# A quarter of the tokens through row gathers in a product-key expert layer

## The chip, the cores and the metric

The kernel runs on one core of a Trainium2 chip. The metric is the device time of one launch in microseconds (us), 2985.03 us as the median of three runs before the change.

## What is computed

The whole layer is an adaptive-LN transformer layer over 512 latent tokens and 256 context tokens of width 1024: a token mixer (Fourier branch and gated DeltaNet branch), a post-norm, and then product-key retrieval of single-neuron experts ("PEER"), with a last post-norm. The change lies in the experts. Each token has 8 heads that pick 16 of 16384 experts each, so 128 experts per token:

```
expert_idx = take_along_axis(cand_i, best_j)          # per token 8 heads x 16 experts
gate = softmax(best_s)
act  = gelu(einsum('td,thkd->thk', h, expert_u[expert_idx]), approximate=False)
coef = gate * act
out  = einsum('thk,thkd->td', coef, expert_v[expert_idx])
x    = post_norm(x, mx[:, 5] * out, ln_g[l, 1], ln_b[l, 1])
```

All arrays are float32. `expert_u` and `expert_v` have 16384 rows of 1024 values (4 KB a row).

## The kernel before

The kernel is one program with a hand-written order for each engine (SP and ACT issue the loads and stores, PE multiplies, ACT, DVE and POOL work element by element), tied together by counting semaphores.

Products with weights use a split: a weight tile of 128 x 1024 values comes from DRAM into `raw` (2 slots), ACT casts it to `w_hi`, POOL subtracts to get `w_lo` (`lo`, L837; 4 slots each), and each product takes three matmuls (`mm3`, L471: hi x hi, lo x hi, hi x lo). The load of tile n + 2 is issued by SP when `split_done` says that POOL is through with tile n (`next_w`). The cast of a tile into a slot of the ring waits until PE is through with the tile four before it.

The experts are computed densely: not 128 per token, but all 16384 for all 512 tokens, 128 tiles of 128 experts each. The stages, in order:

1. Query: 16 rounds. A round multiplies one tile of the query weights and one tile of `peer_u` by the 512 tokens (`lat_hi`, `lat_lo`), 24 matmuls each, then multiplies queries by sub-keys. DVE takes the top 16 of each (L1221 to L1252).
2. Candidates: four blocks of 128 tokens. DVE combines the two key halves, takes the top 16 again, and writes expert indices and gates (`eidx`); ACT gives the exponential after its `U_CD` u tiles of the block (L785). Meanwhile PE runs 8 u tiles a block (`U_CD = 8`); it then waits for `cd_out` and transposes `eidx` (L1709).
3. Marks: 64 rounds of 8 tokens. For each token DVE writes two marks of 128 columns (L1318: 1 where the row of the expert grid is, L1319: the gate where the column is), PE multiplies the two (L1720) into a 128 x 128 table of gates, ACT copies it to `gs`, and it is stored to DRAM (`g_dram`). One u tile runs in each round. The result of every u tile goes through gelu (`gu`) and to DRAM (`gu_dram`).
4. The last 16 u tiles.
5. Values: 128 tiles. DVE multiplies gelu values and gates (`cf`, L1329), ACT and DVE split the product (`c_hi`, `c_lo`), PE multiplies the tile of `peer_v` by it into 8 banks (experts' width as rows, 512 tokens as columns): 24 matmuls of 512 columns. `gl` and `gq` bring gelu values and gates back from DRAM, 1 MB each for four tiles.
6. The end: ACT scales the banks into `acc`, PE transposes it back, DVE adds the residual (L1353), normalizes, and SP stores the output.

## Time and profile before

| | |
|---|---|
| median of 3 runs | 2985.03 us (2984.15 to 2985.14) |
| the profiled execution, its own time | 2981.59 us |
| its span, first to last instruction | 2979.8 us |
| PE busy | 2728.1 us (92%) |
| PE weight loads busy | 2233.9 us (75%) |
| DVE busy | 1433.3 us (48%) |
| POOL busy | 967.3 us (32%) |
| ACT busy | 917.5 us (31%) |
| DMA, mean over the span | 354.24 MB, 119 GB/s |
| share of the span after the query stage begins (1277 us) | 57% |

Matmuls are pipelined, so the mean duration of one (about 0.4 us) is not what it costs. The cost is the distance from one start to the next, which the timeline gives. A busy share is a mean over stages with different limits, so the table is only the way in.

### The profile page before, as it was taken

How to read it: one execution, taken by the hardware profiler on the slowest of the kernel's cores; microseconds unless marked ns; L12 is line 12 of the kernel's file. 1: busy time of each engine (PE TensorE's matmuls, PEld its weight loads, DVE VectorE, ACT ScalarE, POOL GpSimd, SP SyncE). 2: the span in 40 equal slices, each digit the busy share in tenths (PEclk: the TensorE clock that was granted, in tenths of full speed). 3: DMA queues.
4: the chain of work that ended last, by engine and by line, in shares of the span. 5: the costliest groups of instructions: out<-in, count | busy, mean ns of one | idle time of the engine just before them, and what ended most of it. 6: DMA issues, size and time to landing. Idle time of an engine off the chain costs nothing.

```text
span 2979.8 us, 40461 instructions
## 1 busy us (share of the span) xinstructions
PE 2728.1 (92%) x13688; PEld 2233.9 (75%) x13688; DVE 1433.3 (48%) x3468; ACT 917.5 (31%) x1217; POOL 967.3 (32%) x425
## 2 busy tenths in 40 slices
PE   6888889889888999599989999999999999999996
PEld 2687677677667677478877788888878888888885
DVE  2656647647655111434678677777402222222223
ACT  3322221321321222233333445555322222222221
POOL 1212211221220244234444333333344444444441
PEclk8999899899898999799999999999999999999998
DMA  5100100110111223133343355555565555555551
GB/s 208 64 29 28 56 35 34 43 39 31 42 56 36 70 100 102 47 102 111 116 137 115 104 179 204 168 166 209 181 206 179 183 198 182 181 200 179 181 203 50
DMA packets 130236, 354.24 MB, mean 119 GB/s; under 512 B 10640, under 2 KB 43536, under 8 KB 128784
## 3 DMA queue, kind: packets, MB, share of 16 engines
q1 hardware_dynamic: 127648, 312.76, 31.7%
q10 hardware_dynamic: 2544, 40.90, 3.5%
q8 instruction: 28, 0.46, 0.1%
q14 instruction: 16, 0.13, 0.0%
HBM read 284.41 MB, written 69.21 MB: 119 GB/s over the span
## 4 chain that ended last, share of the span: by engine, by line
issue 45%; PE 27%; POOL 18%; DVE 6%; ACT 2%; DMA 0%; POOLq 0%; DVEq 0%; SPq 0%; ACTq 0%
POOL w_lo L840 17%; PE bank L473 4%; PE bank L475 4%; PE bank L474 4%; DVE cv L1014 2%; PE bank L1491 2%; PE bank L1506 2%; PE bank L1499 2%; PE bank L1366 1%; PE bank L1432 1%; DVE dY L1052 1%; PE bank L1422 1%; PE bank L1615 1%; PE bank L1534 1%; PE bank L1541 1%
## 5 line engine op out<-in xcount | busy, mean ns | idle before, releaser
L840 POOL TENSOR_TENSOR w_lo<-raw,w_hi 128x1024 fp32r<-128x1024 f32 x344 | 850.2, 2473 | 1717.8 <-ACT w_hi L709 864.2
L473 PE MATMUL bank<-lat_hi,w_hi 128*128 128x512 f32 x1568 | 631.8, 403 | 22.1 <-DMA sk<-sub_keys 8.1
L475 PE MATMUL bank<-lat_hi,w_lo 128*128 128x512 f32 x1568 | 614.9, 392 | 0.0
L474 PE MATMUL bank<-lat_lo,w_hi 128*128 128x512 f32 x1568 | 614.4, 392 | 0.0
L473 PE MATMUL bank<-c_hi,w_hi 128*128 128x512 f32 x1024 | 405.8, 396 | 6.8 <-ACT gu L766 6.8
L474 PE MATMUL bank<-c_lo,w_hi 128*128 128x512 f32 x1024 | 405.7, 396 | 0.0
L475 PE MATMUL bank<-c_hi,w_lo 128*128 128x512 f32 x1024 | 405.5, 396 | 0.0
L473 PEld LDWEIGHTS bank<-lat_hi,w_hi 128*128 128x128 f32 x1568 | 297.6, 190 | 81.8 <-issue 23.8
L475 PEld LDWEIGHTS bank<-lat_hi,w_lo 128*128 128x128 f32 x1568 | 296.4, 189 | 64.7
L474 PEld LDWEIGHTS bank<-lat_lo,w_hi 128*128 128x128 f32 x1568 | 297.8, 190 | 56.7
L1318 DVE TENSOR_SCALAR oh<-cst,eidT 128x128 f32<-128x128 f32 x512 | 247.1, 483 | 105.2 <-PE bank L1720 103.3
L1329 DVE TENSOR_TENSOR cf<-gl,gq 128x512 f32<-128x512 f32 x128 | 100.8, 788 | 333.6 <-DMA gq<-g_dram 330.1
L709 ACT CAST w_hi<-raw 128x1024 fp32r<-128x1024 f32 x244 | 254.3, 1042 | 0.0
L810 ACT CAST c_hi<-cf 128x512 fp32r<-128x512 f32 x128 | 79.3, 620 | 513.7 <-PE bank L475 502.7
L473 PEld LDWEIGHTS bank<-c_hi,w_hi 128*128 128x128 f32 x1024 | 193.0, 188 | 53.8 <-issue 7.2
L475 PEld LDWEIGHTS bank<-c_hi,w_lo 128*128 128x128 f32 x1024 | 192.9, 188 | 46.5
L474 PEld LDWEIGHTS bank<-c_lo,w_hi 128*128 128x128 f32 x1024 | 192.9, 188 | 46.5
L1335 DVE TENSOR_TENSOR c_lo<-cf,c_hi 128x512 fp32r<-128x512 f32 x128 | 88.3, 690 | 279.0 <-ACT c_hi L810 278.9
L1319 DVE TENSOR_SCALAR oh<-cst,eidT 128x128 f32<-128x128 f32 x512 | 189.6, 370 | 0.0
L1720 PEld LDWEIGHTS bank<-oh 128*128 128x128 f32 x1024 | 125.7, 194 | 8.2 <-issue 3.4
L796 ACT COPY gs<-bank 128x512 f32 x128 | 129.3, 1119 | 0.1
L1720 PE MATMUL bank<-oh 128*128 128x128 f32 x1024 | 126.4, 277 | 3.0 <-DVE oh L1319 3.0
(291 smaller groups left out, 3338.2 us busy)
## 6 DMA issues: line engine op xcount, KB each, us to landing
raw<-w SPq DMA_DIRECT2D x344, 512.0 KB, 3.7
gu_dram<-gu SPq DMA_DIRECT2D x128, 256.0 KB, 3.9
g_dram<-gs ACTq DMA_DIRECT2D x8, 4096.0 KB, 12.4
gl<-gu_dram SPq DMA_DIRECT2D x32, 1024.0 KB, 6.5
gq<-g_dram SPq DMA_DIRECT2D x32, 1024.0 KB, 9.1
ada<-w_ada SPq DMA_DIRECT2D x32, 512.0 KB, 4.0
ada_a<-w_ada SPq DMA_DIRECT2D x8, 512.0 KB, 8.7
xin<-x SPq DMA_DIRECT2D x4, 512.0 KB, 12.1
```

Source lines behind the costliest of these rows:

```text
L473: nc.tensor.matmul(out, hi, rh, start=start, stop=False)
L474: nc.tensor.matmul(out, hi, rl, start=False, stop=False)
L475: return nc.tensor.matmul(out, lo, rh, start=False, stop=stop)
L709: nc.scalar.copy(w_hi[:, q % RING, :], raw[:, q % RAW, :]).then_inc(hi_done, 1)
L796: nc.scalar.copy(gs[:, j, :, bass.ds(t * 32 + (8 * w + 4 * z), 4)].rearrange("p i t -> p t i"), bank[z][:, :].rearrange("p (t i) -> p t i" ...
L810: nc.scalar.copy(c_hi[:, y % 4, :], cf[:, y % 2, :]).then_inc(ch, 1)
L840: nc.gpsimd.tensor_sub(w_lo[:, slot, :], raw[:, slot % RAW, :], w_hi[:, slot, :].bitcast(F32)).then_inc(split_done, 1)
L1318: nc.vector.tensor_scalar(first_, iota, eidT[:, 0, col], None, ALU.is_equal).then_inc(oh_done, 1)
L1319: nc.vector.tensor_scalar(oh[:, z, w, 1, :], iota, eidT[:, 1, col], eidT[:, 2, col], ALU.is_equal, ALU.mult).then_inc(oh_done, 1)
L1329: nc.vector.tensor_tensor(cf[:, x % 2, :].rearrange("p (g t) -> p g t", t=GTOK), gl[:, slot, x % 4, :].rearrange("p (g t) -> p g t", t=GTO ...
L1335: nc.vector.tensor_sub(c_lo[:, x % 4, :], cf[:, x % 2, :], c_hi[:, x % 4, :].bitcast(F32)).then_inc(cl, 1)
L1720: last = mm(bank[z][:, v * P:(v + 1) * P], oh[:, z, v, 1, :], oh[:, z, v, 0, :], start=True, stop=True)
```

## The change

The first 128 of the 512 tokens no longer go through the dense stages. For them POOL issues 256 indirect gathers (`fetch`): gather q brings, for each of the 128 tokens, the row of its q-th expert (128 rows of 4 KB, 512 KB), first 128 times from `peer_u`, then 128 times from `peer_v`, into a ring of `ROWS = 8` buffers. DVE takes the dot product of each u row with the token (`dot`, the token rows lie in PSUM, `pair`), ACT applies one gelu to all of them (`e_act`), and DVE adds each v row times its coefficient into `pair` in PSUM (`add_row`).

The other 384 tokens (`DT`) go through the dense stages: u matmuls have 384 columns. The candidate blocks take 12 u tiles each (`U_CD = 12`), the marks stage has 48 rounds, the tail again 16. In the marks stage DVE reads its iota from a PSUM bank (`bank[5]`), not from SBUF, and writes the first mark of four tokens in one instruction. In the values stage the roles are swapped: coefficients (128 tokens) are the weights and a tile of `peer_v` is what moves, 512 columns at a time, 18 matmuls a tile, so the sums lie with tokens as rows. The end needs no scaling by ACT and no transposes; DVE multiplies by a gate row (`g2row`, made before by two matmuls with ones) and adds the residual. Coefficients and gelu values come back in transfers of 768 KB.

```diff
+DT = SEQ - P
+U_CD = 12
-X_END = X_G + SEQ // 8
+X_END = X_G + DT // 8
+ROWS = 8
+DOT_G = 8 * (DT // 32)
+V_BANK = ((0, 1), (4, 5), (6, 7))
...
+            def fetch(q):
+                if q == 0:
+                    pool.wait_ge(row_id, 1)
+                if q >= ROWS and q % 2 == 0:
+                    pool.wait_ge(row_used, q - ROWS + 2)
+                table = A["peer_u"] if q < P else A["peer_v"]
+                nc.gpsimd.indirect_dma_start(rows[:, q % ROWS, :], None, table,
+                                             bass.IndirectOffsetOnAxis(ap=e_row[:, q % P:q % P + 1], axis=0)
+                                             ).then_inc(row_in[q % ROWS // 2], 16)
+            def tile_of(q):
+                if q < ROWS:
+                    return T_U - 2 * PH + X_CD + 2 * U_CD + RING
+                n = q - ROWS
+                if n < DOT_G:
+                    return T_U - 2 * PH + X_G + n // 2 + RING + 1
+                if n < P:
+                    return T_U - 2 * PH + X_END + RING + 1 + (n - DOT_G) // 3
+                return T_V + n - P + RING + 1
+            q = 0
+            for n in range(T_QUERY + RING, T_ALL):
+                lo(n % RING, n + 1)
+                while q < 2 * P and tile_of(q) <= n:
+                    fetch(q)
+                    q += 1
...
-            with dve.Fori(0, SEQ // 8) as t:
-                for z in range(2):
-                    dve.wait_ge(g_mm, t * 2)
-                    for w in range(4):
-                        col = bass.ds(t * 8 + (4 * z + w), 1)
-                        first_ = oh[:, z, w, 0, :]
-                        nc.vector.tensor_scalar(first_, iota, eidT[:, 0, col], None, ALU.is_equal).then_inc(oh_done, 1)
-                        nc.vector.tensor_scalar(oh[:, z, w, 1, :], iota, eidT[:, 1, col], eidT[:, 2, col],
-                                                ALU.is_equal, ALU.mult).then_inc(oh_done, 1)
+            def dot(i, q):
+                if q % 2 == 0:
+                    dve.wait_ge(row_in[q % ROWS // 2], i * 32 + (q // ROWS + 1) * 32)
+                row = rows[:, q % ROWS, :]
+                nc.vector.scalar_tensor_tensor(row, row, 1.0, pair[:, :], ALU.mult, ALU.mult,
+                                               accum_out=e_dot[:, bass.ds(i * ROWS + q, 1)]).then_inc(row_used, 1)
+            def marks(t, g):
+                z = g % 2
+                own = slice(4 * z, 4 * z + 4)
+                cols = bass.ds(t * 32 + 4 * g, 4)
+                nc.vector.tensor_tensor(hole_i[:, own, 0:P], rep(bank[5][:, 0:P], 4), bc(eidT[:, 0, cols], P),
+                                        ALU.is_equal).then_inc(oh_i_done, 1)
+                for v in range(4):
+                    col = bass.ds(t * 32 + (4 * g + v), 1)
+                    nc.vector.tensor_scalar(hole_j[:, 4 * z + v, 0:P], bank[5][:, 0:P], eidT[:, 1, col], eidT[:, 2, col],
+                                            ALU.is_equal, ALU.mult).then_inc(oh_j_done, 1)
...
+            def add_row(i, x, first):
+                if x % 2 == 0:
+                    dve.wait_ge(row_in[x // 2], i * 32 + (P // ROWS + 1) * 32)
+                dve.wait_ge(row_used, i * ROWS + (P + x))
+                weight = e_coef[:, bass.ds(i * ROWS + x, 1)]
...
+                    nc.vector.scalar_tensor_tensor(pair[:, :], rows[:, x, :], weight, pair[:, :], ALU.mult,
+                                                   ALU.add).then_inc(row_used, 1)
...
                 for k in range(KB):
-                    last = mm3(bank[6 + x % 2][:, :], *w_block(n % RING, k), lat_hi[:, k, :], lat_lo[:, k, :],
+                    last = mm3(bank[6 + x % 2][:, 0:DT], *w_block(slot, k), lat_hi[:, k, P:], lat_lo[:, k, P:],
                                k == 0, k == KB - 1)
...
-                for k in range(KB):
-                    last = mm3(bank[k][:, :], *w_block(y % RING, k), c_hi[:, y % 4, :], c_lo[:, y % 4, :], start, stop)
+                for t in range(DT // P):
+                    if t == DT // P - 1 and start:
+                        pe.wait_ge(gelu, PK)
+                    own = slice(t * P, (t + 1) * P)
+                    parts = ((c_hi, w_hi), (c_hi, w_lo), (c_lo, w_hi))
+                    for n, (c_, w_) in enumerate(parts):
+                        for e in range(2):
+                            last = mm(bank[V_BANK[t][e]][:, :], c_[:, y % 4, own], w_[:, y % RING, e * 512:(e + 1) * 512],
+                                      start=start and n == 0, stop=stop and n == 2)
```

How the engines' orders move is seen at three places. POOL of the changed program, first where the gathers begin (`w_lo` is the split of a weight tile, `rows` the ring of gathered rows), then from the end of the tail into the values stage; before, POOL has only the `w_lo` rows here:

```order
L874 TENSOR_TENSOR w_lo<-raw,w_hi 128x1024 x57
L944 DMA rows<-peer_u,e_row 128x1024 x8
L874 TENSOR_TENSOR w_lo<-raw,w_hi 128x1024 x25
L944 DMA rows<-peer_u,e_row 128x1024 x2
L874 TENSOR_TENSOR w_lo<-raw,w_hi 128x1024
```

```order
L944 DMA rows<-peer_u,e_row 128x1024 x3
L874 TENSOR_TENSOR w_lo<-raw,w_hi 128x1024
L944 DMA rows<-peer_v,e_row 128x1024 x3
L874 TENSOR_TENSOR w_lo<-raw,w_hi 128x1024
L944 DMA rows<-peer_v,e_row 128x1024 x3
L874 TENSOR_TENSOR w_lo<-raw,w_hi 128x1024
L944 DMA rows<-peer_v,e_row 128x1024 x2
L874 TENSOR_TENSOR w_lo<-raw,w_hi 128x1024 x6
L944 DMA rows<-peer_v,e_row 128x1024
L874 TENSOR_TENSOR w_lo<-raw,w_hi 128x1024
```

Two gathers stand behind each split in the marks stage, three behind each of 11 splits in the tail (the last 8 of them already of `peer_v`), one in the values stage.

DVE, marks stage, two of the 16 marks of a round before (`oh` the marks, `cst` holds the iota; an ISA row is a wait):

```order
L1312 ISA
L1318 ISA
L1318 TENSOR_SCALAR oh<-cst,eidT 128x128
L1319 ISA
L1319 TENSOR_SCALAR oh<-cst,eidT 128x128
```

and a whole round in the changed program (`hole_i`, `hole_j` the marks, `bank` the PSUM bank with the iota):

```order
L1397 TENSOR_TENSOR hole_i<-bank,eidT 128x4x128
L1401 TENSOR_SCALAR hole_j<-bank,eidT 128x128 x4
L1397 TENSOR_TENSOR hole_i<-bank,eidT 128x4x128
L1401 TENSOR_SCALAR hole_j<-bank,eidT 128x128 x4
L1388 SCALAR_TENSOR_TENSOR rows,e_dot<-rows,pair 128x1024 x2
```

Ten mark instructions take the place of sixteen, and two dot products of 1024 columns stand behind them.

DVE, one tile of the values stage in the changed program; before it is the two rows of `c_lo` and `cf` with 512 columns:

```order
L1433 REGISTER_ALU
L1434 TENSOR_TENSOR c_lo<-cf,c_hi 128x384
L1428 TENSOR_TENSOR cf<-gl,gq 128x384
L1442 REGISTER_ALU
L1447 ISA
L1447 SCALAR_TENSOR_TENSOR pair<-rows,e_coef,pair 128x1024
```

One instruction of 1024 columns, with a wait ahead of it, is added to each tile; the other two have 384 columns.

## Rows read from the trace of the kernel before

**Rows 1.** The page: busy us by engine (share of the span), instructions.
```profile
PE 2728.1 (92%) x13688; PEld 2233.9 (75%) x13688; DVE 1433.3 (48%) x3468; ACT 917.5 (31%) x1217; POOL 967.3 (32%) x425
```

**Rows 2.** Windows by stage: length, busy (instructions), granted clock, DMA share, GB/s.
```profile
1277.00:1463.00 186.00, 186.00 (x885) 156.09 (x884) 89.00 (x570) 65.10 (x86) 74.33 (x31) 1.00 0.35 109
1463.00:1663.00 200.00, 182.87 (x779) 149.35 (x777) 154.34 (x370) 63.09 (x82) 88.10 (x33) 0.95 0.42 126
1663.00:2129.00 466.00, 463.38 (x2543) 401.96 (x2544) 359.25 (x1024) 240.44 (x271) 150.48 (x63) 0.99 0.50 169
2129.00:2227.00 98.00, 91.24 (x402) 75.00 (x400) 6.56 (x10) 27.98 (x39) 37.71 (x17) 0.98 0.66 225
2227.00:2945.00 718.00, 717.94 (x3070) 578.44 (x3071) 179.66 (x246) 195.34 (x249) 318.78 (x126) 1.00 0.53 179
2945.00:2980.00 35.00, 6.36 (x36) 5.26 (x34) 22.36 (x33) 4.74 (x8) 1.01 (x1) 0.68 0.15 60
```

**Rows 3.** Timeline of PE, marks stage: start, us, instruction.
```profile
1764.33 0.48 PE L473 MATMUL bank<-lat_hi,w_hi 128*128 128x512 f32 x1
...
1769.88 1.95 PE L1720 MATMUL bank<-oh 128*128 128x128 f32 x16
1771.59 0.48 PE L473 MATMUL bank<-lat_hi,w_hi 128*128 128x512 f32 x1
```

**Rows 4.** Timeline of PE, 256-column matmuls of an earlier stage.
```profile
281.88 0.28 PE L475 MATMUL bank<-ctx_hi,w_lo 128*128 128x256 f32 x1
...
282.58 0.28 PE L475 MATMUL bank<-ctx_hi,w_lo 128*128 128x256 f32 x1
```

**Rows 5.** The copy behind each block's transposes: ns, first and last start.
```profile
L787 ACT COPY eidT<-bank x4: 479/479/483, 1511.3 to 1662.7; 128x384 f32 x4
```

**Rows 6.** Timeline of DVE and POOL, one round of the marks stage.
```profile
1764.73 2.28 DVE L1318 TENSOR_SCALAR oh<-cst,eidT 128x128 f32<-128x128 f32 x1 [1.64 <-PE bank L1720]
1766.93 0.33 DVE L1319 TENSOR_SCALAR oh<-cst,eidT 128x128 f32<-128x128 f32 x1
...
1770.09 0.34 DVE L1319 TENSOR_SCALAR oh<-cst,eidT 128x128 f32<-128x128 f32 x1
1764.52 2.41 POOL L840 TENSOR_TENSOR w_lo<-raw,w_hi 128x1024 fp32r<-128x1024 f32 x1 [4.93 <-ACT w_hi L804]
```

**Rows 7.** Groups of instructions by shape: DVE on wider tiles, POOL large and small.
```profile
L1353 DVE SCALAR_TENSOR_TENSOR xo<-x,bank 128x512 f32<-128x512 f32 x8 | 5.0, 683 | 27.8 <-PE bank L1750 27.8
L1201 DVE TENSOR_TENSOR xo<-xo,gb 128x1024 f32<-128x1024 f32 x4 | 4.6, 1217 | 0.0
L840 POOL TENSOR_TENSOR w_lo<-raw,w_hi 128x1024 fp32r<-128x1024 f32 x344 | 850.2, 2473 | 1717.8 <-ACT w_hi L709 864.2 <-ACT w_hi L599 531.8 <-ACT w_hi L804 321.8
L907 POOL TENSOR_TENSOR rstd<-vare,nhalf 128x4 f32<-128x4 f32 x1 | 1.0, 1007 | 35.6 <-DVE vare L1188 35.6
L832 ACT ACTIVATE acc<-bank,mods 128x512 f32<-128x512 f32 x8 | 4.7, 704 | 20.8 <-PE bank L475 20.8
```

**Rows 8.** DMA issues, values stage: KB each, us from issue to landing.
```profile
gq<-g_dram SPq DMA_DIRECT2D x30, 1024.0 KB, 9.1
...
raw<-w SPq DMA_DIRECT2D x1, 512.0 KB, 6.9
raw<-w SPq DMA_DIRECT2D x1, 512.0 KB, 3.1
```

**Rows 9.** Timeline of ACT, DVE and SP's issues, values stage.
```profile
2520.80 1.04 ACT L709 CAST w_hi<-raw 128x1024 fp32r<-128x1024 f32 x1
2525.91 0.69 DVE L1329 TENSOR_TENSOR cf<-gl,gq 128x512 f32<-128x512 f32 x1
2526.52 0.69 DVE L1335 TENSOR_TENSOR c_lo<-cf,c_hi 128x512 fp32r<-128x512 f32 x1
2541.28 0.35 SPq L487 DMA_DIRECT2D raw<-w  x1
```

**Rows 10.** DMA: bytes and mean rate at the start of the program (10 to 30 us).
```profile
DMA packets 2256, 8.24 MB, mean 412 GB/s; under 512 B 245, under 2 KB 245, under 8 KB 2256
```

More of the change, by code:

```diff
@@ L1323, in coefficients @@
+            for q in range(DOT_G, P):
+                dot(0, q)
             def coefficients(i, x):
@@ L1691, in _ @@
                     pe.wait_ge(gelu, i * 4 + max(j - 1, 0))
[L1692 to L1695 removed]
+                    scores_u(j, (2 * j + 1) % RING)
                     pe.wait_ge(q_ev, i * 4 + (j + 1))
```

278 lines of the change are left out of this document (179 added, 99 removed).

## The prediction

> **What bounds the kernel now.** I read the page's busy times first, then the windows by stage, then the timeline in each stage for the distance between starts, and last the transfers. The page shows PE busy 92% and its weight loads 75%, DVE at half, POOL and ACT at a third [rows 1]: PE is the suspect, but a mean over stages. The windows say where [rows 2]: from the query stage on, PE is busy 186 of 186 us, 183 of 200 in the candidate blocks, 463 of 466 in the marks, 91 of 98 in the tail and 718 of 718 in the values stage, at a granted clock of 0.95 to 1.00, the upper level (2.4 GHz). These five stages are 1668 us. Only the end (35 us) is not PE's. So a change that takes columns from PE pays in full, until something else becomes slower than PE. That is the whole question here.
>
> A u tile is 24 matmuls of 512 columns in 5.55 us (1764.33 to 1769.88), 231 ns each; the marks of a round add 1.71 us [rows 3]. The values stage has 718 / 128 = 5.61 us a tile, 234 ns a matmul [rows 2].
>
> **The price of a narrower matmul.** A matmul might not get cheaper with fewer columns, if the weight load, about 0.16 to 0.19 us busy (2233.9 / 13688 = 163 ns, [rows 1]), set the pace. It doesn't: 256-column matmuls start 117 ns apart (six steps from 281.88 to 282.58, [rows 4]). Between 117 and 231, 384 columns cost 174 ns, a u tile 4.2 us. In the values stage the width stays 512 and 24 become 18: 18 x 234 = 4.2 us. These are PE's floors.
>
> **The price of a gather.** Nothing in the trace shows one. Call f the time that POOL needs to issue one. The lower end is SP's issue of a plain transfer, 0.35 us [rows 9]; the upper end is a POOL operation over 1024 columns, 2.47 us [rows 7]. A gather handles one index per partition, so it is nearest to POOL's small operation, 1.0 us [rows 7], plus an issue: I take f = 1.3. For its first byte alone the Trainium skill (DMA: Bandwidth & Descriptors, Specifications) gives about 1 us on the GpSimd path; no run here shows it yet, and with f = 1.0 the sum below would be lower by 10 us, in the tail alone.
>
> **Part by part**, against the profiled execution, 2981.6 us (3.4 below the median).
>
> *Query stage.* 16 u tiles lose 5.55 - 4.2 = 1.35 us each: -22 us. Query tiles stay whole. DVE is busy 89 of 186 us [rows 2], so it stays covered.
>
> *Candidate blocks.* The copies behind the blocks' transposes start from 1511.3 to 1662.7, so a block takes 50.5 us [rows 5]: 8 x 5.55 = 44.4, and 6.1 in which PE waits for the exponential, which ACT does behind the last u tile, for DVE and for the transposes. The wait is tied to the last tile, so it stays with 12 tiles: 12 x 4.2 + 6.1 = 56.5, three times; the first block has no transposes, 50.4. Sum 220 instead of 200: +20, for 16 more tiles done. DVE, busy 154 of 200 [rows 2], fits.
>
> *Marks stage.* 48 rounds instead of 64. PE needs 4.2 + 1.7 = 5.9 us. DVE: marks start 0.226 us apart now (14 steps from 1766.93 to 1770.09, [rows 6]); if they now pass one element a cycle like the wide ones (690 ns for 512 columns [rows 9], 1217 for 1024 [rows 7], so 1.03 ns a column), 64 columns' worth is added, 0.07 us, and I allow 0.03 for the PSUM operand: 8 x 0.32 = 2.6. Two marks of 512 columns: 0.61 from start to start [rows 9], 1.2. Two dot products of 1024 columns: 1217 ns less the 0.08 that starts overlap, 2.3. With hand-overs 0.2: 6.3 us. POOL: 2.4 + 2 x 1.3 = 5.0. Transfers of a round: tile 512 KB, gelu values 192, gates 512, two gathers 1024, about 2.3 MB: 5.6 us at the 412 GB/s that the start reaches [rows 10], 6.8 at the 338 that a full share is worth here (169 / 0.50, [rows 2]). So DVE leads narrowly, with PE, POOL and transfers all within 1.3 us: 48 x 6.3 = 302 against 466, -164 us.
>
> What makes this possible is that the first mark of a round now takes 2.28 us, not 0.27: it starts 0.2 us behind POOL's split and lasts until that ends [rows 6]. The marks of the changed program read their iota from PSUM, so they no longer share POOL's way to SBUF; I take it that the 2 us go. The Trainium skill (SBUF — State Buffer, Who interferes with whom) says that only a DVE operation in a two-port mode, or with two SBUF inputs beside a POOL operation that reads SBUF, is locked out. By that rule, the trace agrees as to the lock, and the new marks would be free; if the lock stays, see the rivals.
>
> *Tail.* 16 tiles. POOL has 3 gathers behind 11 splits: 2.4 + 3.9 = 6.3 us against PE's 4.2. 11 x 6.3 + 5 x 4.2, plus the 9 us by which 98 exceeds 16 x 5.55 now, minus some 8 because POOL runs up to four tiles ahead: 91 against 98, -7 us. The 32 dot products of the tail, 36 us on DVE, fit, but the first coefficients are queued behind them.
>
> *Values stage.* PE's floor is 4.2. DVE has 2 x 0.5 + 1.15 plus waits, under 3 us; POOL 2.5 + 1.3 = 3.8. The next limit is the raw slot: load, cast 1.04 [rows 9], split 2.47 [rows 7], then the next load into the same slot. The slot that is loaded behind `gl` and `gq` sees 6.9 us, then 3.1 us [rows 8]: 10.0 + 2 x (1.04 + 2.47 + 0.15) = 17.3 us for four tiles, 4.3 a tile. At 5.6 us that is hidden; at 4.2 it isn't. The smaller bursts (1.5 MB instead of 2 in 9.1 us, [rows 8]) take about 1 us off; a gather of 512 KB beside each load adds up to 1.27 each at 412 GB/s [rows 10]. So 16.3 to 18.9, or 4.1 to 4.7 a tile. I take 4.5: 576 against 718, -142 us.
>
> *The end.* Scaling by ACT (4.7 us, [rows 7]) and the transposes go; DVE gets two more passes per token block of 512 columns at 0.68 [rows 7], but two of three dense blocks come before PE's last matmul: -5 us. The gate row's two matmuls, DVE's diagonal and the 8 extra transposes lie where PE waits for the norms (6 of the last 35 us busy shows how such a stretch looks, [rows 2]); without that cover they cost 3 us.
>
> Sum: -22 + 20 - 164 - 7 - 142 - 5 = -320, so 2981.6 - 320 = 2662 and **2665 us** as a median.
>
> **Rivals.**
> *PE stays the bound everywhere.* Marks 48 x 5.9 = 283 (-183), tail 76 (-22), values 538 (-180): -392, 2593 us. For it: DVE's margin in the marks is thin. Against: the slot chain of the values stage.
> *POOL or the transfers take over.* With f = 2.5 the marks round is 7.4 (355, -111), the tail 131 (+33), a values tile 5.05 (646, -72): -157, 2828 us. A transfer system that gives only 338 GB/s gives 6.8 in the marks, which alone is 24 us. For it: every stage adds traffic beside the loads, and POOL's gathers stand in the way of the next split.
> *The lock stays on the marks.* Another 2 us in each of 48 rounds: +96, 2761 us. Against it is the one-port form of the operands.
> *Slower.* One mechanism: POOL's issue. The three stages cost 115 + 96 f, 48 + 33 f and 326 + 128 f, together 489 + 257 f; 1282 us now, and the rest gains 7: it turns slower from f = 3.1 us. At 3.5 the time is 3085 us. Nothing in the trace excludes it, as 128 descriptors of 4 KB have to be written one way or another, but it is three times the small operation of [rows 7].
> *The change doesn't do what it says*: the order shows 384 columns and 18 matmuls, so I give it nothing.
>
> **Numbers.** Forecast 0.46, PE everywhere 0.15, POOL or transfers 0.23, lock 0.08, slower 0.08. A measurement of this kernel tells about 0.2% (6 us) from no change. Faster 0.91, same 0.01, slower 0.08. The range 2580 to 2840 takes in the PE floor and f = 2.5, and leaves out the slower case and a little beyond either end.
>
> **What would show it.** Matmuls of 384 columns 174 ns apart; marks rounds of 6.3 us with DVE busy over 90% and no mark of 2 us; tail tiles of 6.3 us with POOL back to back; values tiles of 4.2 to 4.7 us in which PE waits for POOL's split every fourth tile, and raw loads of 4 to 7 us; the row of a gather's issue. The prediction is wrong if POOL's split waits for gathers by more than 2 us, if 384 columns cost as much as 512, or if PE waits for DVE in the values stage.

## The result and the profile after

The changed kernel takes 2828.07 us (median of 4 runs, 2822.35 to 2836.64) against 2985.09 us: ratio 0.948, 95% interval 0.9466 to 0.9493. It is 157 us faster, about half of the 320 us forecast. The profiled execution took 2836.64 us, its span 2834.8; it is the longest of the four, 8.6 us over the median, so the stage lengths below are those of a somewhat long execution.

The page of the changed kernel, its busy times and two rows of the 40 slices (granted clock, DMA share):

```profile
PE 2409.3 (85%) x12641; PEld 2054.1 (72%) x12641; DVE 1639.6 (58%) x3319; ACT 817.0 (29%) x1175; POOL 1220.8 (43%) x681
...
PEclk9998998998998999979999889999999899999998
DMA  5200101101101122313345547888898777777773
```

PE went from 92% [rows 1] to 85%: its work shrank more than the time did. The windows by stage, cut at the same events as [rows 2] and with the same columns (query, candidate blocks, marks, tail, values):

```profile
1280.00:1448.00 168.00, 168.00 (x899) 153.20 (x898) 91.16 (x582) 64.45 (x88) 76.51 (x32) 1.00 0.36 115
1448.00:1691.00 243.00, 206.84 (x1144) 203.03 (x1143) 155.70 (x364) 80.23 (x110) 139.87 (x57) 0.94 0.53 163
1691.00:2040.00 349.00, 300.53 (x1909) 297.81 (x1910) 289.39 (x669) 131.97 (x202) 197.68 (x137) 0.92 0.79 290
2040.00:2145.00 105.00, 76.21 (x397) 72.47 (x395) 39.39 (x67) 22.40 (x32) 72.03 (x54) 0.92 0.98 369
2145.00:2808.00 663.00, 575.64 (x2304) 459.03 (x2304) 416.18 (x392) 195.89 (x256) 436.06 (x246) 0.92 0.75 267
```

| stage | before, us | forecast | after | after against forecast |
|---|---|---|---|---|
| query | 186 | 164 | 168 | +4 |
| candidate blocks | 200 | 220 | 243 | +23 |
| marks | 466 | 302 | 349 | +47 |
| tail | 98 | 91 | 105 | +14 |
| values | 718 | 576 | 663 | +87 |
| end | 35 | 30 | 27 | -3 |

172 us are missing in these rows; with 3 us that the query stage begins later, that is 2834.8 less the forecast's span of about 2660. In all four stages where they are missing PE is no longer busy throughout and the granted clock is 0.92 to 0.94; in the query stage, where PE has no gap, it is 1.00. DMA is at a share of 0.53 to 0.98, where [rows 2] had 169 GB/s at 0.50 in the marks.

**Marks.** The waits of 1690 to 2038 us, two of the long pieces of the chain of waits there, the timeline around the second of them (each engine from its own view), and the first marks of two rounds between such pieces:

```profile
ACT gu L837 <- DMA gu_dram<-gu: 67.4, 8, 12.1
DVE rows L1388 <- DMA rows<-peer_u,e_row: 58.2, 12, 12.1
...
PE bank L1868 <- DVE hole_j L1401: 50.6, 7, 11.1
```

```profile
1741.65 17.52 DMA rows<-peer_u,e_row
...
1801.70 17.16 DMA rows<-peer_u,e_row
```

```profile
1807.98 1.95 PE L1868 MATMUL bank<-hole_i,hole_j 128*128 128x128 f32 x16
...
1818.99 1.22 DVE L1388 SCALAR_TENSOR_TENSOR rows<-rows,pair 128x1024 f32<-128x1024 f32 x1 [10.84 <-DMA rows<-peer_u,e_row]
...
1822.62 0.49 ACT L837 ACTIVATE gu<-bank 128x384 f32<-128x384 f32 x1 [10.68 <-DMA gu_dram<-gu]
...
1823.29 3.91 PE L1868 MATMUL bank<-hole_i,hole_j 128*128 128x128 f32 x16 [9.20 <-DVE hole_j L1401]
```

```profile
1761.58 0.69 DVE L1397 TENSOR_TENSOR hole_i<-bank,eidT 128x512 f32<-128x512 f32 x1
...
1767.61 0.69 DVE L1397 TENSOR_TENSOR hole_i<-bank,eidT 128x512 f32<-128x512 f32 x1
```

Gathers take 17 us instead of their median of 6.3, some 60 us apart. Two more of 17 us follow at 1860.89 and 1920.86, and a fifth of 19 us at 1980.69. Each stands beside one of ACT's 4 MB stores of the gate table (`g_dram`), issued at 1742.55, 1802.59, 1861.90, 1921.81 and 1981.69, which land after 17.6 us. DVE waits for the gather with its dot product, its marks are queued behind that, and PE waits for the marks 9 us. From the starts of `hole_i`, most rounds take 6.03 us (1761.58 to 1767.61; DVE busy throughout, so it leads), and just five take 15.8 to 18.3. So 48 x 6.1 and five times 10.8 us are 347 of the 349. Behind the stall the 16 matmuls of the marks take 3.91 us where they took 1.95 before it: the granted clock is 0.50 from 1817 to 1827 us, the lower level (1.2 GHz), and 1.00 from 1806 to 1814, while PE was busy throughout.

**Candidate blocks.** The waits of 1448 to 1691 us:

```profile
ACT gu L794 <- DMA gu_dram<-gu: 136.6, 41, 15.4
...
DVE bf L1368 <- ACT bf L814: 81.6, 4, 34.7
...
PE bank L1856 <- DVE eidx L1373: 20.3, 3, 7.3
```

A loop that the forecast has nowhere: gelu of a tile writes into the slot of the tile two before it and waits for that one's store; SP issues the store only behind `next_w`, which waits for POOL's split, which waits for ACT's cast, which stands behind the gelu. Gelu 0.49, cast 1.04, split 2.4 (with a gather beside it 3), SP 0.6, landing 3.6 (4.6 in the median of the whole run): 8.5 to 9 us for two tiles, 4.3 to 4.5 a tile. At 5.55 us a tile it was hidden, at 4.2 it isn't. And `exp` is done behind the twelfth tile though DVE had its input ready at about the fifth (1521 of a block from 1503 to 1554 us).

**Values.** The waits of 2145 to 2807 us, then one group of four tiles (SP's two reloads; DVE's wait for them; PE behind that wait; POOL's wait for the late tile):

```profile
DVE cf L1428 <- DMA gq<-g_dram: 233.8, 31, 9.3
...
ACT w_hi L733 <- DMA raw<-w: 192.1, 104, 5.9
...
PE bank L1887 <- DVE c_lo L1434: 92.3, 30, 6.6
```

```profile
2502.20 0.38 SPq L579 DMA_DIRECT2D gq<-g_dram  x1
...
2512.68 0.56 DVE L1428 TENSOR_TENSOR cf<-gl,gq 128x384 f32<-128x384 f32 x1 [7.68 <-DMA gq<-g_dram]
...
2514.96 1.22 PE L1887 MATMUL bank<-w_hi,c_hi 128*128 128x512 f32 x2 [4.55 <-DVE c_lo L1434]
2515.98 1.05 PE L1887 MATMUL bank<-w_lo,c_hi 128*128 128x512 f32 x2
2516.83 1.05 PE L1887 MATMUL bank<-w_hi,c_lo 128*128 128x512 f32 x2
...
2515.57 2.38 POOL L874 TENSOR_TENSOR w_lo<-raw,w_hi 128x1024 fp32r<-128x1024 f32 x1 [6.19 <-ACT w_hi L733]
...
2522.89 0.38 SPq L579 DMA_DIRECT2D gq<-g_dram  x1
```

A group takes 20.7 us (2502.20 to 2522.89) against 16.8 that PE needs. `gq` is issued at 2502.2, DVE stops for it at 2505.0 and gets it at 2512.7. `gl` and `gq` take 7.6 and 10.8 us to land, a tile's load 3.1 to 11.5.

The stall costs more than its own length. Before it, two matmuls of 512 columns start every 0.46 us; behind it, every 0.85 us (2515.98 to 2516.83), until 2519.4. The granted clock is 1.00 from 2500 to 2510 us, while PE is busy throughout, and 0.50 from 2515 to 2519, behind a stall of 4.55 us. In the whole stage PE is busy 574.6 us, and 535.0 for the same 2300 recorded matmuls in a run below (no_v_gather) that has hardly a stall and a clock of 1.00.

What the prediction said would show: 384 columns at 174 ns, marks without a lock, and the gather's issue at 0.94 us (`peer_u`) and 1.06 us (`peer_v`) plus 0.16 to 0.3 of gap all came. DVE was not over 90% in the marks (83%), and values tiles took 5.18 us, not 4.2 to 4.7. In the values stage PE waits 92.3 us in 30 waits for `c_lo`, which is DVE's, and not for POOL's split: "if PE waits for DVE in the values stage" is one of the signs that the prediction named for being wrong.

### The profile page after: what moved, and what is told of

It reads as the page before. It is cut to its first block, busy times and chain, and to the rows that moved or that the text cites. A ratio compares the mean times of both kernels' runs of the same rounds, so it can differ in the third digit from the quotient of the medians.

```text
span 2834.8 us, 37454 instructions
## 1 busy us (share of the span) xinstructions
PE 2409.3 (85%) x12641; PEld 2054.1 (72%) x12641; DVE 1639.6 (58%) x3319; ACT 817.0 (29%) x1175; POOL 1220.8 (43%) x681
## 4 chain that ended last, share of the span: by engine, by line
PE 45%; DMA 18%; POOL 16%; DVE 10%; issue 5%; ACT 5%; SPq 1%; DVEq 1%; ACTq 0%; POOLq 0%
POOL w_lo L874 12%; DMA raw<-w 10%; PE bank L498 8%; PE bank L500 7%; PE bank L499 7%; DMA rows<-peer_u,e_row 4%; DMA gu_dram<-gu 4%; POOL rows L944 4%; DVE cv L1075 3%; PE pair L1623 2%; PE bank L1638 2%; PE bank L1868 2%; PE bank L1631 2%; ACT w_hi L733 2%; DVE dY L1113 1%
## 5 line engine op out<-in xcount | busy, mean ns | idle before, releaser
L498 PE MATMUL bank<-lat_hi,w_hi 128*128 128x384 f32 (+1 forms) x1536 | 566.0, 368 | 56.1 <-ACT gu L794 36.0
L500 PE MATMUL bank<-lat_hi,w_lo 128*128 128x384 f32 (+1 forms) x1536 | 548.9, 357 | 0.0
L499 PE MATMUL bank<-lat_lo,w_hi 128*128 128x384 f32 (+1 forms) x1536 | 548.7, 357 | 0.0
L1887 PE MATMUL bank<-w_hi,c_hi 128*128 128x512 f32 x768 | 257.8, 419 | 93.7 <-DVE c_lo L1434 92.3
L733 ACT CAST w_hi<-raw 128x1024 fp32r<-128x1024 f32 x260 | 271.9, 1046 | 192.9 <-DMA raw<-w 192.1
L499 PEld LDWEIGHTS bank<-lat_lo,w_hi 128*128 128x128 f32 x1536 | 294.6, 192 | 17.6
L1887 PE MATMUL bank<-w_lo,c_hi 128*128 128x512 f32 x768 | 252.0, 411 | 0.0
L1887 PE MATMUL bank<-w_hi,c_lo 128*128 128x512 f32 x768 | 251.8, 411 | 0.0
L1434 DVE TENSOR_TENSOR c_lo<-cf,c_hi 128x384 fp32r<-128x384 f32 x128 | 191.5, 1496 | 0.1
L1887 PEld LDWEIGHTS bank<-w_lo,c_hi 128*128 128x128 f32 x768 | 153.7, 200 | 35.3
L1887 PEld LDWEIGHTS bank<-w_hi,c_lo 128*128 128x128 f32 x768 | 153.2, 200 | 35.3
L1447 DVE SCALAR_TENSOR_TENSOR pair<-rows,e_coef,pair 128x1024 f32<-128x1024 f32 x127 | 162.8, 1282 | 0.2
L1868 PE MATMUL bank<-hole_i,hole_j 128*128 128x128 f32 x768 | 106.7, 297 | 50.7 <-DVE hole_j L1401 50.6
L944 POOL DMA_INDIRECT rows<-peer_v,e_row x128 | 135.0, 1055 | 20.6 <-issue 15.1
## 6 DMA issues: line engine op xcount, KB each, us to landing
g_dram<-gs ACTq DMA_DIRECT2D x6, 4096.0 KB, 17.6
gq<-g_dram SPq DMA_DIRECT2D x32, 768.0 KB, 10.8
```

The source lines that it names most:

```text
L498: nc.tensor.matmul(out, hi, rh, start=start, stop=False)
L499: nc.tensor.matmul(out, hi, rl, start=False, stop=False)
L500: return nc.tensor.matmul(out, lo, rh, start=False, stop=stop)
L733: nc.scalar.copy(w_hi[:, q % RING, :], raw[:, q % RAW, :]).then_inc(hi_done, 1)
L944: nc.gpsimd.indirect_dma_start(rows[:, q % ROWS, :], None, table, bass.IndirectOffsetOnAxis(ap=e_row[:, q % P:q % P + 1], axis=0)).then_in ...
L1434: nc.vector.tensor_sub(c_lo[:, x % 4, :], cf[:, x % 2, :], c_hi[:, x % 4, :].bitcast(F32)).then_inc(cl, 1)
```

## Experiments

All times below are medians, with the ratio to the kernel before and its 95% interval. Stage lengths are from the profiled execution of each, cut where DVE begins the first candidate block, where the first and last marks are, and where the values' first and last matmuls begin. Cut so, the changed kernel has 236, 348, 107 and 662 us. In stages that an edit doesn't touch the executions differ: blocks 231 to 236, marks 340 to 348, tail 104 to 108, values 650 to 668. So a move of under 8 us in the marks or 18 us in the values says nothing by itself, and there the time of the whole kernel has to tell. Bold is the stage that an edit aims at.

| kernel | us | ratio | blocks | marks | tail | values |
|---|---|---|---|---|---|---|
| the change | 2828.1 | 0.948 (0.947 to 0.949) | 236 | 348 | 107 | 662 |
| store_first | 2800.1 | 0.938 (0.936 to 0.940) | **220** | 340 | 107 | 650 |
| exp_early | 2808.9 | 0.942 (0.939 to 0.945) | **214** | 342 | 107 | 653 |
| spread | 2829.5 | 0.949 (0.945 to 0.952) | **230** | 340 | 106 | 664 |
| paced | 2795.9 | 0.936 (0.934 to 0.938) | 236 | **311** | 104 | 665 |
| iota_sbuf | 2857.1 | 0.956 (0.955 to 0.958) | 236 | **367** | 105 | 668 |
| early_back | 2817.9 | 0.944 (0.943 to 0.946) | 232 | 345 | 106 | **647** |
| paced_back | 2752.3 | 0.922 (0.921 to 0.924) | 231 | 341 | 106 | **582** |
| no_v_gather | 2702.1 | 0.905 (0.903 to 0.906) | 236 | 347 | 101 | **543** |
| quarter_rows | 2702.2 | 0.905 (0.904 to 0.907) | 233 | **303** | **98** | **583** |
| one_sbuf | 2840.7 | 0.951 (0.949 to 0.953) | 235 | 348 | 108 | **666** |
| all_paced | 2670.7 | 0.894 (0.893 to 0.896) | **195** | **306** | **102** | **590** |
| all_earlier | 2671.1 | 0.893 (0.891 to 0.895) | **196** | **311** | **103** | **582** |

### The candidate blocks: store_first, exp_early, spread

```diff
                 for j in range(4):
+                    store_gu(i * 4 + (2 * PH - 4), j)
                     next_w(i * 4, T_U + j)
-                    store_gu(i * 4 + (2 * PH - 4), j)
```

> Edit: in the u loop SP issues the store of gelu values ahead of the wait for the next weight load, not behind it. Theory 'order' (in the candidate blocks gelu of tile x waits for the store of tile x-2, which SP issues only behind POOL's split; that loop makes 4.4 to 4.6 us a tile): the 41 waits of 136.6 us in total on gu_dram there mostly go, the candidate blocks fall from 243 us towards 48 x 4.2 + 18 for the ends of the blocks + some 10 for one long stall = 230 us, the time to about 2815 us. Theory 'transfers' (the landing itself is what is late, whatever is issued first): the waits move to the raw loads, the blocks stay within 4 us of 243, the time at 2828 us.

The gelu no longer waits for stores; in 1452 to 1672 us it waits for PE, as it should, and some loads are late instead:

```profile
ACT gu L794 <- PE bank L500: 83.0, 37, 2.8
...
ACT w_hi L733 <- DMA raw<-w: 41.2, 24, 12.7
```

The blocks lose 16 us, where 13 were expected (243 to 230, cut as in the table of stages above). The theory of the order holds: by the other one the blocks would have stayed within 4 us. The time falls by 28 us, more than the blocks give. The loop that the edit changes also runs in the marks and the tail, where the five long rounds now take 13.3 to 16.0 us and the tail stays at 107; the values stage, at 650, is within what untouched ones differ by. What the other 12 us are is not shown.

```diff
                     hi_n(T_U + RING + j, b, U_CD)
-                act.wait_ge(cd, b * CD_N + CD_EXP)
-                nc.scalar.activation(bf[5][:, :, :], bf[4][:, :, :], ACT.Exp).then_inc(cd_exp, 1)
+                    if j == 7:
+                        act.wait_ge(cd, b * CD_N + CD_EXP)
+                        nc.scalar.activation(bf[5][:, :, :], bf[4][:, :, :], ACT.Exp).then_inc(cd_exp, 1)
```

> Edit: in each candidate block ACT does the exponential behind the 8th of 12 u tiles, not behind the 12th. Theory 'order': DVE has its input ready at about the 5th tile, so the 81.6 us in which DVE waits for the exponential halve, and PE's wait for eidx (20.3 us, three blocks) goes; the end of each block keeps only transposes, about -5 us each in three blocks and -3 in the last: candidate blocks 243 to about 228, time about 2812 us. Rival: the wait of PE moves to the stores and loads behind it, since the blocks are led by the loop through the stores: under 5 us gained, time 2823 us or more.

The blocks fall by 22 us, where 15 were expected. The wait of DVE for `exp` goes from 81.6 to 18.9 us while gelu still waits as before:

```profile
ACT gu L794 <- DMA gu_dram<-gu: 133.1, 43, 10.1
...
DVE bf L1369 <- ACT bf L815: 18.9, 2, 11.1
```

PE's wait for `eidx`, 20.3 us before, is gone from the list. So most of the prediction's 6.1 us at the end of each block was tied to the last tile only by the place of one instruction (22 us in four blocks are 5.5 each).

```diff
-                    return T_U - 2 * PH + X_CD + 2 * U_CD + RING
+                    return T_U - 2 * PH + X_CD + 2 * U_CD + RING + 2 * q
```

> Edit: the first eight gathers, issued one behind the other within 11 us of the third block (4 MB), are issued two tiles apart. In the changed kernel one gelu waits 15.4 us for its store in just that stretch, against 2 to 4 us elsewhere. Theory 'burst': this one wait falls below 6 us and the candidate blocks from 236 to 224 to 228 us, time about 2818 us. Rival: ring and stores hide it, the blocks stay within 4 us, 2828 us.

The longest wait of a gelu falls from 15.4 to 6.6 us, the blocks by 6 us, hardly more than untouched ones differ by, and the time not at all. The burst of eight gathers is real but worth little alone.

### The marks: paced, iota_sbuf

```diff
-                    act.dma_start(g_dram[i * 2 + j], gs[:, j, :, :]).then_inc(gs_st[j], 16)
+            def store_piece(s, p):
+                act.dma_start(g_dram[s][:, p * 32:(p + 1) * 32, :], gs[:, s % 2, p * 32:(p + 1) * 32, :]).then_inc(gs_st[s % 2], 16)
...
+                    if s and r in (0, 2, 4, 6):
+                        store_piece(s - 1, (0, 2, 4, 6).index(r))
```

(ACT's loop over the rounds is written out, s is the slot of 8 rounds and r the round in it, so the pieces of one slot go out in the rounds of the next.)

> Edit: each of the six 4 MB stores of the gate table is issued as four stores of 1 MB, two rounds apart; the bytes stay. Theory 'burst' (a store of 4 MB at once holds back the raw loads, the gathers and the stores of gelu values by 9 to 10 us, six times; 349 us = 48 x 6.0 + 6 x 10): the marks stage falls to 295 to 315 us, the time to 2775 to 2795 us. Theory 'bytes' (2.3 MB a round are simply more than the transfers carry beside each other): the pieces only spread the same loss, the stage stays within 10 us of 349, the time over 2815 us. Should the loss be DVE's alone, as the forecast of 6.3 us a round has it, the stage ends at 302 us and DVE is busy over 90%.

The marks stage in its window (columns as above):

```profile
1687.00:1998.00 311.00, 293.35 (x1898) 287.59 (x1899) 290.21 (x671) 117.80 (x191) 196.23 (x137) 0.99 0.89 321
```

311 us, as the theory of the burst has it. PE waits for marks 18.3 us, not 50.6, and 2.7 at most, not 11.1. The longest round is now 8.9 us, not 18.3. The bytes are the same and now flow at 321 GB/s, share 0.89, so the stage was not out of bandwidth at 290. The clock is 0.99 again instead of 0.92. DVE is busy 290 of 311 us: without the stalls it is the leader that the prediction took it for.

```diff
-                nc.vector.tensor_tensor(hole_i[:, own, 0:P], rep(bank[5][:, 0:P], 4), bc(eidT[:, 0, cols], P),
+                nc.vector.tensor_tensor(hole_i[:, own, 0:P], rep(iota, 4), bc(eidT[:, 0, cols], P),
...
-                    nc.vector.tensor_scalar(hole_j[:, 4 * z + v, 0:P], bank[5][:, 0:P], eidT[:, 1, col], eidT[:, 2, col],
+                    nc.vector.tensor_scalar(hole_j[:, 4 * z + v, 0:P], iota, eidT[:, 1, col], eidT[:, 2, col],
```

> Undoes one part of the change: the marks read their iota from SBUF again, not from the PSUM bank; widths, counts and waits stay. Theory 'lock' (the forecast's): marks with all operands in SBUF wait for POOL's split, one in a round takes 2 us, DVE leads, and the marks stage gains up to 2 us in each of 48 rounds: 348 to 400 to 440 us, less where the wait lies in one of the six long stalls; time 2880 to 2920 us. Theory 'transfers' (the stage is led by the bursts, DVE's 83% leaves room): under 15 us more, time below 2845 us.

The marks in the view of one tile's instructions (ns at least, in the median, at most): the first mark of each group with the iota in PSUM, then first and second marks with the iota in SBUF, each from its own kernel:

```profile
L1397 DVE TENSOR_TENSOR hole_i<-bank,eidT x96: 679/686/714, 1689.5 to 2034.4; 128x512 f32<-128x512 f32 x96
```

```profile
L1397 DVE TENSOR_TENSOR hole_i<-cst,eidT x96: 678/689/2893, 1688.4 to 2052.6; 128x512 f32<-128x512 f32 x96
L1401 DVE TENSOR_SCALAR hole_j<-cst,eidT x384: 331/341/3108, 1689.0 to 2054.0; 128x128 f32<-128x128 f32 x192
```

Both theories miss. The lock is real: marks of up to 3.1 us come back, and none is above 0.71 us with the iota in PSUM. But DVE's busy time in the stage rises by 31 us and the stage by 19, not by 52 to 92: most marks don't meet the split. Reading the iota from PSUM is worth 19 us in its stage and 29 in the whole (2857.1 less 2828.1), under a third of the 96 that the rival had.

### The values: early_back, no_v_gather, quarter_rows, one_sbuf, paced_back

```diff
-                    if y == 1 and not first:
-                        sp_.wait_ge(cf_done, r_ * 8)
-                        load_gl(r_ * 2 + 1, 1)
-                        load_gq(r_ * 2 + 1, 1)
+                    if y == 7 and not last:
+                        sp_.wait_ge(cf_done, r_ * 8 + 8)
+                        load_gl(r_ * 2 + 3, 1)
+                        load_gq(r_ * 2 + 3, 1)
-                    if y == 5 and not last:
+                    if y == (5 if first else 3) and not last:
```

> Edit: in the values stage the loads of gl and gq (1.5 MB for four tiles) are issued two tiles earlier. Theory 'order' (they are issued just when DVE needs them, so each group of four tiles waits for their landing): the 31 waits of DVE's cf on gq, 234 us in total, fall below 60 us, a group of four tiles takes 17.5 to 18.5 us, not 20.7, the values stage 560 to 595 us, not 663, the time 2725 to 2760 us. Theory 'transfers' (16 queues are shared by loads, gathers and reloads, and the split waits for raw): the wait on gq goes but comes back at raw, the stage stays over 640 us, the time over 2800 us.

A miss for the theory of the order. The wait for `gq` shrinks, though not below the 60 us expected, and another grows by more (2134 to 2781 us):

```profile
ACT w_hi L733 <- DMA raw<-w: 436.9, 115, 9.2
...
DVE cf L1428 <- DMA gq<-g_dram: 86.0, 30, 4.9
...
PE bank L1887 <- POOL w_lo L874: 79.4, 34, 4.7
```

The stage is 15 us shorter, which is no more than untouched stages differ by; the time falls by 10. By the theory of the transfers the stage stays over 640 us, as it does, and the time over 2800. Asking earlier for 1.5 MB in one piece delays the next tile's load; PE now waits 79 us for POOL's split of that tile in place of 92 for `c_lo`. Each group has two chains, one through `gq` and one through the raw slot, and shortening one lets the other end last.

```diff
-                while q < 2 * P and tile_of(q) <= n:
+                while q < P and tile_of(q) <= n:
...
-            for q in range(q, 2 * P):
-                fetch(q)
...
-                if x % 2 == 0:
-                    dve.wait_ge(row_in[x // 2], i * 32 + (P // ROWS + 1) * 32)
```

> Leaves out the 128 gathers of peer_v rows: DVE adds whatever the row buffers hold, all else stays, so the first 128 tokens come out wrong and the time is that of the changed kernel without 64 MB of gathers and without POOL's 1.1 us for each. Theory 'slot chain' (a raw load behind gl and gq lands 10 us late or more, because gathers share the queues with it, and holds cast, split and next load back): loads land in 3 to 8 us again, a group of four tiles takes 17 to 18 us instead of 20.7, the values stage falls from 662 to 545 to 580 us. Theory 'late issue' (what counts is that gl and gq are asked for too late): only their landing gets shorter, from 10.7 to some 8.5 us, a group takes 18.5 us or more, the stage 590 to 620 us. If neither holds and the clock or the split of c_lo leads, the stage stays over 640 us.

```profile
2136.00:2679.00 543.00, 535.03 (x2300) 431.02 (x2301) 455.36 (x389) 189.64 (x255) 320.07 (x126) 1.00 0.61 211
```

```profile
ACT w_hi L733 <- DMA raw<-w: 6.2, 10, 4.3
```

```profile
gl<-gu_dram SPq DMA_DIRECT2D x30, 768.0 KB, 5.4
gq<-g_dram SPq DMA_DIRECT2D x30, 768.0 KB, 7.7
```

543 us is PE's floor (128 x 4.2 = 538), at a clock of 1.00, though `gl` and `gq` are issued as late as before; they land in 5.4 and 7.7 us, not 7.6 and 10.7, and ACT's wait for loads all but goes. So without the gathers the late reloads cost nothing. Of the 119 us gained, 79 are idle time of PE (662 less 574.6, against 543 less 535.0) and 40 are busy time, at a clock of 1.00 in place of 0.92. This run doesn't say whether it is the gathers' bytes or POOL's time; the next does.

```diff
+                width = D if q < ROWS else D // 4
+                table = table.rearrange("n (a d) -> (n a) d", a=D // width) if width < D else table
-                nc.gpsimd.indirect_dma_start(rows[:, q % ROWS, :], None, table,
+                nc.gpsimd.indirect_dma_start(rows[:, q % ROWS, 0:width], None, table,
```

(The dot product's factor is 0.001 in place of 1.0, to keep the repeated use of old columns finite.)

> Changes the computation: every gather but the first eight brings 1 KB a row instead of 4 (128 descriptors as before, 128 KB instead of 512), DVE still goes over 1024 columns. Theory 'bytes' (what the gathers cost is their transfer): marks stage 348 to below 320 us, tail 107 to below 92, values 662 to below 610, time 2700 to 2760 us. Theory 'issue' (what they cost is POOL's 0.94 to 1.10 us and its place ahead of the split): no stage moves by more than 10 us, time over 2805 us.

POOL's cost of a gather stays, and two waits shrink, for `gq` from 233.8 us and for loads from 192.1 (2089 to 2672 us; this run's profile has no landing times for these transfers):

```profile
L946 POOL DMA_INDIRECT rows<-peer_v,e_row x120 | 128.5, 1071 | 18.7 <-issue 15.4
```

```profile
DVE cf L1430 <- DMA gq<-g_dram: 159.4, 31, 7.2
ACT w_hi L733 <- DMA raw<-w: 130.8, 95, 2.2
```

Marks -45, values -79 us, with the same 256 gathers issued: a gather costs mainly by its bytes. In the marks the five long rounds are 8.4 to 9.9 us now, the others 6.03 as before: it takes the gathers' bytes and the store's together to stall the stage for 10 us and more. A gather's issue on POOL, the term f on which the slower rival stood, is at most the 40 us between 583 and 543 in the values stage. In the tail the gain is 9 us, less than expected (98 against below 92): gelu still waits 59.6 us for its stores there. The order of SP doesn't explain that by itself: store_first, whose edit runs in the tail too, cut that wait from 71.5 to 21.9 us and left the tail at 107. What holds the tail once the gathers are light is open.

```diff
+                dve.wait_ge(row_used, P if isinstance(i, int) and i == 0 and x < 3 else i * 8 + (P + x))
                 nc.vector.tensor_sub(c_lo[:, x % 4, :], cf[:, x % 2, :],
-                                     c_hi[:, x % 4, :].bitcast(F32)).then_inc(cl, 1)
+                                     pair[:, 0:DT]).then_inc(cl, 1)
```

(The added wait is for DVE's own earlier work on `pair`, so the waits do not stay quite as they were.)

> Changes the computation: DVE's c_lo subtracts a PSUM operand of the same width in place of c_hi in SBUF, so it has one SBUF input; count, width and waits stay. c_lo takes 1.50 us on average now, 0.55 at least and 1.95 in the median, since it shares the way to SBUF with POOL's split. Theory 'lock': c_lo falls to about 0.55 us and the 92 us in which PE waits for c_lo with it, the values stage by 25 us or more. Theory 'loads' (c_lo is last only because cf waited for gq 7.7 us before it): c_lo falls to 0.55 us, but the stage by less than 15 us: the chain of a group is 20.7 us long through the loads, and one c_lo of it saves 1.4 us x 31 groups at most, if PE starts behind it, and otherwise nothing.

DVE's groups, of 2145 to 2670 us:

```profile
L1428 DVE TENSOR_TENSOR cf<-gl,gq 128x384 f32<-128x384 f32 x102 | 114.3, 1120 | 225.8 <-DMA gq<-g_dram 223.1
...
L1435 DVE TENSOR_TENSOR c_lo<-cf,pair 128x384 fp32r<-128x384 f32 x101 | 55.9, 554 | 3.8
```

`c_lo` falls from 1.50 to 0.55 us, but `cf`, which has two inputs in SBUF too, rises from 0.61 to 1.12. Which of the two meets POOL's split depends on when they run: in no_v_gather, where `c_lo` is untouched, `cf` takes 1.67 us on average and `c_lo` 0.80. The stage stays (666 against 662), as the theory of the loads has it. That PE waits for `c_lo` in the list of waits says who came last, not why: `c_lo` is late since `cf` was.

```diff
+            def piece(q, slot, m):
...
+                    if y in (3, 4, 5) and not last and not first:
+                        piece(r_ * 2 + 2, 0, y - 3)
```

(Piece 0 is `gq` of four of the six gate slots, piece 1 the other two and `gl` of one tile, piece 2 `gl` of three tiles. The second slot's pieces are issued at y = 7, 0 and 1; the plain calls of `load_gl` and `load_gq` go.)

> Edit: the 1.5 MB of gl and gq for a group of four tiles are issued in three pieces of about 0.5 MB, one tile apart, the first two tiles earlier than in the changed kernel. Asking for them two tiles earlier in one piece gained 15 us in the values stage: DVE's wait for gq fell from 234 to 86 us, ACT's wait for raw loads rose from 192 to 437. Theory 'slot chain' (the raw load behind the burst is what holds the stage): each raw load now shares with a third of the burst, lands in 5 to 8 us each, none over 9, a group takes 17.5 to 18.5 us and the stage 560 to 595 us. Theory 'bytes' (5.5 MB in four tiles, at a DMA share of 0.75 to 0.77, are what is left, however cut): the stage stays over 630 us.

```profile
ACT w_hi L746 <- DMA raw<-w: 177.0, 91, 4.9
...
DVE cf L1441 <- DMA gl<-gu_dram: 122.2, 31, 6.0
```

582 us, 18.2 a group, from the same bytes: both chains are shorter at once, where early_back had only traded one for the other. PE's idle time falls from 87 to 31 us (662 - 575 and 582 - 551), and its busy time from 575 to 551 for the same matmuls, at a clock of 0.98. The stage and the length of a group are as the theory of the slot chain has them; the landing times that it forecast are not in this run's profile.

### Together: all_paced, all_earlier

> The changed kernel with all edits that gained one by one: stores of gelu values issued first, the exponential behind the 8th tile, gate table stored in pieces of 1 MB, gl and gq brought back in three pieces, and the first eight gathers two tiles apart instead of in one burst of 4 MB. Each alone moved its stage: blocks 236 to 220 and to 214 us, marks 348 to 311, values 662 to 582. Theory 'queues' (each stage lost to a burst or an order of its own, so the gains add, except that the two in the blocks cover in part the same wait): blocks 201 to 210, marks 300 to 311, tail 98 to 107, values 575 to 585: 2834.8 - 30 - 40 - 3 - 80 = 2680 us, range 2665 to 2700. Theory 'one pool of bytes' (what one stage sheds the next one gets, or the clock falls with higher activity): less than 120 us gained in all, over 2705 us.

```profile
1454.00:1649.00 195.00, 192.59 (x1113) 191.94 (x1111) 161.45 (x333) 83.08 (x109) 147.01 (x54) 1.00 0.61 193
1649.00:1956.00 307.00, 292.29 (x1897) 286.92 (x1898) 289.81 (x671) 116.76 (x190) 198.26 (x138) 0.99 0.90 328
1956.00:2057.00 101.00, 77.47 (x409) 74.82 (x407) 40.41 (x69) 24.51 (x33) 73.70 (x54) 0.91 1.02 397
2057.00:2648.00 591.00, 550.94 (x2303) 433.08 (x2304) 465.27 (x391) 191.84 (x256) 436.87 (x246) 0.99 0.86 300
```

2670.7 us, 157 us below the changed kernel and within its expected range, though the blocks are shorter (201 to 210 expected) and the values longer (575 to 585). The gains add: the single edits gave 28, 19, 32 and 76 us, and -1 for the spread gathers, 154 together. In the blocks PE is busy 193 of 195 us. The forecast was 2665 us, and this is 0.2% from it, for a kernel that does the same work in another order of issue and with more and smaller transfers. So near a hit is luck in part. The stages do not match one by one: the blocks are 25 us under the forecast's 220 (the exponential was moved, which the forecast did not have), and marks, tail and values are 5, 10 and 15 us over its 302, 91 and 576.

```diff
-                    if y in (3, 4, 5) and not last and not first:
-                        piece(r_ * 2 + 2, 0, y - 3)
+                    if y1 <= y < y1 + 3 and not last:
+                        piece(r_ * 2 + 2, 0, y - y1)
```

(y1 is 2, in the first round 4. The second slot's pieces go at y = 6, 7 and 0; the second group's first pieces behind the first loads of `peer_v`.)

> The kernel all_paced (2670.7 us) with the pieces of gl and gq issued one tile earlier still, and at the start of the values stage the second group's pieces behind the first loads of peer_v instead of ahead of them. There, DVE's cf waits for gl in 30 of the groups, 115 us in total or 3.8 us a group, and PE 38 us for c_lo; the first group waits 20 us for the first 3 MB. Theory 'late piece' (the last piece lands just after DVE is ready for it): the waits for gl halve or go, the values stage falls from 590 to 560 to 578 us and the gap ahead of it by some 5 us: 2640 to 2660 us. Theory 'bytes' (queues are at a share of 0.86 and an earlier piece only makes raw loads later, as with early_back): the stage stays over 583 us, 2663 us or more.

```profile
ACT w_hi L746 <- DMA raw<-w: 338.9, 112, 6.2
...
DVE cf L1447 <- DMA gl<-gu_dram: 91.9, 23, 10.2
```

2671.1 us, no difference from all_paced. The time is as the theory of the bytes has it (2663 or more); the stage of 582 us lies between the two theories and within what untouched stages differ by. The wait for `gl` falls from 115 to 92 us, the one for loads rises from 168 to 339: the same trade as in early_back. What is left over the floor is then 582 to 590 against 543, and it isn't settled here how much of it is POOL's 1.1 us a gather, how much the queues and how much the clock behind the stalls that are left (PE busy 551 and 546 us, not 535).

## Why the prediction was right and wrong

**Right.** *PE's floors.* 384 columns at 174 ns and 18 matmuls of 512 columns: the query stage is within 4 us, and with the gathers of `peer_v` gone the values stage is 543 us against the 538 computed. *The gather's issue.* f = 1.3 us was taken, some 1.2 measured with the gap. With it the slower rival, which needed 3.1, is out. The Trainium skill (DMA: Bandwidth & Descriptors, Specifications) gives about 1 us as the latency to the first byte on the GpSimd path. That is another quantity than POOL's busy time of 0.94 and 1.06 us, and no run here shows the first byte, so the nearness of the two numbers confirms nothing. *The lock of the marks.* It went with the iota's move to PSUM: 714 ns at most for a first mark against 2893. The Trainium skill (SBUF — State Buffer, Who interferes with whom) has it so; the trace agrees. *The marks round.* 6.3 us with DVE leading was forecast, 6.03 measured between the stalls; the stage is 303 us with light gathers and 311 with paced stores, against 302. *The sign.*

**Wrong: the size, 157 us instead of 320.** Five steps. In the first three a chain of waits through a transfer was left out or priced as a mean; the fifth follows from them.

1. "48 x 6.3 = 302". The stores of the gate table were put into a round as their mean, 512 KB. They are bursts of 4 MB, and while one flows a gather takes 17 us and the round 10 to 12 us longer, five times. The stage is 47 us over the forecast, and pacing the same bytes returns 37.
2. "I take 4.5: 576". The raw slot's chain was the right limit to look at, but the bursts' share was priced at 6.9 us less 1 plus 1.27 for a gather beside it, and a late load takes up to 11.5. The other chain, `gl` and `gq` issued when DVE is about to need them, was not looked at: 10.8 us to land. Measured 5.18 us a tile; three pieces instead of one bring 4.55, about what the forecast had. DVE, priced at under 3 us a tile with waits, is busy 3.25 (416 / 128), since `c_lo` takes 1.50 us beside POOL's split and not 0.5; one_sbuf shows that this cost the stage nothing.
3. "The wait is tied to the last tile, so it stays with 12 tiles", and +20 for the blocks. It was +43. The loop gelu, cast, split, store of 4.3 to 4.5 us a tile was hidden under 5.55 and was not listed. The exponential's place was costing more than the forecast's 6.1 a block could show: moving it saved 22 us of the stage.
4. "91 against 98". The tail was 105. Forecast as POOL's, 6.3 us a tile. POOL is busy 72 of 105 us, so it doesn't lead; the transfers are at a share of 0.98, and a quarter of the gathers' bytes brings 98. How the rest of the 14 us comes about is not shown.
5. "These are PE's floors." They hold at a granted clock of 1.00. The forecast left the clock at that and had no term for its fall behind a stall. In the values stage, at 0.92, PE is busy 40 us longer for the same matmuls than at 1.00 (574.6 and 535.0), which is nearly half of the 87 us by which that stage is over the forecast. It follows from the stalls of step 2: paced_back, which only issues the reloads otherwise, returns 24 of the 40.

The rival that POOL or transfers take over gave 2828 us, and that is the time measured, but not by its way: it rested on f = 2.5. Of its two halves transfers were right, and 338 against 412 GB/s was not the question either: paced, the marks stage carries 321 GB/s and is not held up by it, unpaced it was held up at 290. That the two numbers agree is luck.

The range, 2580 to 2840, holds the result, near its upper end. PE everywhere (2593) was not reached by any version.

## What to carry to other kernels

When a change makes the leading engine a quarter faster, list every loop that passes through a store or a reload and a slot, with its length, also those that the profile of before shows as idle time that cost nothing: the first one longer than the new period sets the pace. Price a burst as a burst: for as long as it flows, everything behind it lands late, and cutting it in pieces one or two tiles apart gave back 32 and 76 us here with no byte less. Where PE leads, a stall costs more than its length: behind the stalls PE also ran at the lower clock, which came to 40 of 662 us here. A wait that only moves when its transfer is asked for earlier (`gq` -148 us, loads +245 us) is a sign of two chains on one set of queues.
